# Expert loop of a mixture-of-experts block: a gate chunk split ahead of the rows, and the result rows copied by one engine

## The reference, cut to what matters

```
def hier_moe(h, ...):                 # 512 tokens, D = 1024
    g_sel = argmax(h @ w_rg + b_rg)   # 4 groups
    top_v, top_i = top_k(e_logit of that group's 8 experts, 2)
    gate = softmax(top_v) * g_p
    ...                               # tokens sorted by expert, blocks of 128 rows
    def expert_block(xb, e):          # 32 experts, inner width 512
        return (silu(xb @ w_gate[e]) * (xb @ w_up[e])) @ w_down[e]
    out[token] += expert_block(...) * gate
x = x + hier_moe(rms_norm(x), ...)
```

## Time and profile before

| | |
|---|---|
| median of 3 runs | 3697.85 us (3696.06 to 3704.15) |
| profiled execution | 3699.9 us |
| its span, first to last instruction | 3698.1 us |
| PE busy | 3507.7 us, 95% |
| DVE busy | 2201.3 us, 60% |
| ACT busy | 1511.9 us, 41% |
| POOL busy | 423.4 us, 11% |
| moved by DMA | 522.35 MB, mean 141 GB/s |

### The profile page before, as it was taken

The page is one execution under the profiler, slowest core; times in us unless marked ns, Lnnn a source line. Parts: engine busy times, 40 slices in busy tenths (PEclk is TensorE's granted clock), DMA queues, the critical chain, the costliest instruction groups (busy, mean ns, idle before and its releaser), DMA issues. The chain is left out here.

```text
span 3698.1 us, 44707 instructions
## 1 busy us (share of the span) xinstructions
PE 3507.7 (95%) x17472; PEld 2876.0 (78%) x17472; DVE 2201.3 (60%) x2966; ACT 1511.9 (41%) x1709; POOL 423.4 (11%) x315
## 2 busy tenths in 40 slices
PE   8999999899899999999999999899997997999998
PEld 6888888655888888888758888877876866887786
DVE  7545446538654467557897433653226326999998
ACT  4111111547422232223445222544545235777775
POOL 2000000200110011001111100100000011444442
PEclk9999999999999999999999999999999997999999
DMA  6323323210244335444212232231222226999997
GB/s 258 122 81 104 113 89 102 65 57 1 80 148 137 117 100 182 154 153 149 69 33 68 94 103 83 72 130 52 86 86 74 92 82 227 355 355 352 357 369 299
DMA packets 315240, 522.35 MB, mean 141 GB/s; under 512 B 18516, under 2 KB 274561, under 8 KB 289216
## 3 DMA queue, kind: packets, MB, share of 16 engines
q1 hardware_dynamic: 304032, 507.06, 39.9%
q0 software_dynamic: 11040, 12.91, 1.1%
HBM read 519.91 MB, written 25.17 MB: 147 GB/s over the span
## 5 line engine op out<-in xcount | busy, mean ns | idle before, releaser
L531 PE MATMUL banks<-operand_hi,trunk_weights_hi 128*128 128x512 f32 (+1 forms) x1568 | 569.2, 363 | 32.8 <-DVE operand_lo L1088 10.7
L531 PE MATMUL banks<-operand_lo,trunk_weights_hi 128*128 128x512 f32 (+1 forms) x1568 | 559.9, 357 | 0.0
L531 PE MATMUL banks<-operand_hi,trunk_weights_lo 128*128 128x512 f32 (+1 forms) x1568 | 559.6, 357 | 0.0
L531 PEld LDWEIGHTS banks<-operand_hi,trunk_weights_hi 128*128 128x128 f32 x1568 | 300.5, 192 | 81.3 <-issue 29.7
L531 PEld LDWEIGHTS banks<-operand_hi,trunk_weights_lo 128*128 128x128 f32 x1568 | 300.6, 192 | 41.7
L531 PEld LDWEIGHTS banks<-operand_lo,trunk_weights_hi 128*128 128x128 f32 x1568 | 300.7, 192 | 41.2 <-issue 0.5
L4249 DVE TENSOR_TENSOR ex_w_lo<-weight_ring,ex_w_hi 128x2048 fp32r<-128x2048 f32 x128 | 288.9, 2291 | 41.5 <-ACT ex_w_hi L4181 41.5
L1316 DVE TENSOR_TENSOR trunk_weights_lo<-weight_ring,trunk_weights_hi 128x2048 fp32r<-128x2048 f32 x90 | 206.4, 2294 | 177.2 <-ACT trunk_weights_hi L1271 177.2
L1271 ACT ACTIVATE trunk_weights_hi<-weight_ring 128x2048 fp32r<-128x2048 f32 x90 | 171.7, 1907 | 216.5 <-PE banks L531 216.3
L4181 ACT ACTIVATE ex_w_hi<-weight_ring 128x2048 fp32r<-128x2048 f32 x128 | 241.7, 1913 | 22.1 <-PE banks L4089 22.1
L531 PE MATMUL banks<-trunk_hidden_hi,trunk_weights_hi 128*128 128x512 f32 (+1 forms) x672 | 233.4, 347 | 4.6 <-DVE X L1818 2.1
(11 more groups left out here) (612 smaller groups left out, 7394.5 us busy)
## 6 DMA issues: line engine op xcount, KB each, us to landing
weight_ring<-ffn_w SPq DMA_DIRECT2D x120, 1024.0 KB, 5.2
weight_ring<-w_mod SPq DMA_DIRECT2D x72, 1024.0 KB, 5.1
weight_ring<-w_gate SPq DMA_DIRECT2D x64, 1024.0 KB, 6.8
weight_ring<-w_up SPq DMA_DIRECT2D x64, 1024.0 KB, 7.6
room<-w_down SPq DMA_DIRECT2D x64, 1024.0 KB, 7.1
weight_ring<-w_in SPq DMA_DIRECT2D x26, 1024.0 KB, 5.2
weight_ring<-ffn_w SPq DMA_DIRECT2D x16, 768.0 KB, 4.5
weight_ring<-o_w_pw SPq DMA_DIRECT2D x8, 1024.0 KB, 5.4
```

What stands on the lines that cost most here:

```text
L531: ins = pe.matmul(bank[:, at:at + width], w, x[:, at:at + width], start=start and n == 0, stop=stop and n == len(passes) - 1)
```

## The change

In `step`, ACT splits GATE0 of the next expert straight behind UP1, then the turned token rows, then GATE1, and only then copies the result rows, all 1024 columns in one instruction. DVE's copy of Y and its semaphore go; DVE makes the low part of GATE0 ahead of that of the token rows. PE's order in the step is the same.

For expert 0 the two UP chunks go to the slots (2, 1) in place of (1, 2), so that UP0 has a free slot from the start and UP1 waits for the gate product; the two halves of its matrix change places with that. The transposes of X and the copies to `XR` move from ahead of the loop to behind it, around the last `turn_h`; ACT alone copies them, in five banks in turn, and DVE waits for them before its first addition.

```
-def load_expert_chunk(k, sp, c, e):
-    half = c % 2
+FIRST_UP = (2, 1)
+def load_expert_chunk(k, sp, c, e, other=0):
+    half = (c + other) % 2
...
-        XRT = lambda j: k.PS[3 - j // 2][:, 512 * (j % 2):512 * (j % 2) + 512]
+        XRT = lambda j: (k.PS[0][:, 0:512], k.PS[0][:, 512:], k.PS[3][:, 512:], G, U)[j % 5]
...
 # POOL, scatter
                 pool.wait_ge(s_ya, m * 2 + (u + 2))
-                pool.wait_ge(s_yd, m * 2 + (u + 2))
...
 # PE: the transposes of X leave the start of the block, and
             step(n, 1, more=False)
+            for j in range(3):
+                turn_rows(j)
             turn_h(n, 2)
+            for j in range(3, 2 * ST):
+                if j >= 5:
+                    pe.wait_ge(s_xra, j - 4)
+                turn_rows(j)
             down(n, 2, DOWN[0])
...
 # ACT
             def rows_out(m, u):
                 act.wait_ge(s_mm, nth(m, u, DOWN[1]))
                 act.wait_ge(s_free[(u + 1) % 2], m + (u - 1) // 2 + 1)
-                act.activation(YS[:, (u + 1) % 2, 0:512], Y[:, 0:512], ACT.Copy).then_inc(s_ya, 1)
+                act.activation(YS[:, (u + 1) % 2, :], Y[:], ACT.Copy).then_inc(s_ya, 1)
...
                 chunk_hi(m, u, UP[1])
+                if more:
+                    chunk_hi(m, u + 1, GATE[0])
+                    turned_x(m, u + 1)
+                    chunk_hi(m, u + 1, GATE[1])
                 rows_out(m, u)
-                if more:
-                    turned_x(m, u + 1)
-                    chunk_hi(m, u + 1, GATE[0])
-                    chunk_hi(m, u + 1, GATE[1])
                 chunk_hi(m, u + 1, DOWN[0], 1 if more else 3)
-            for j in range(0, 2 * ST, 2):
-                act.wait_ge(s_xr, j + 1)
-                act.activation(XR[:, j // 2, 0:512], XRT(j), ACT.Copy).then_inc(s_xra, 1)
             chunk_hi(0, 0, GATE[0])
             chunk_hi(0, 0, GATE[1], 3)
             turned_x(0, 0)
-            chunk_hi(0, 0, UP[0])
+            chunk_hi(0, 0, UP[0], slot=FIRST_UP[0])
+            chunk_hi(0, 0, UP[1], slot=FIRST_UP[1], used=GATE[1] + 1)
             turned_x(0, 1)
             silu(0, 0)
-            chunk_hi(0, 0, UP[1])
...
             step(n, 1, more=False)
+            for j in range(3):
+                rows_of_x(j)
             turned_h(n, 2)
             chunk_hi(n, 2, DOWN[1])
+            for j in range(3, 2 * ST):
+                rows_of_x(j)
...
 # DVE
                 chunk_lo(m, u, UP[1])
-                rows_out(m, u)
                 if more:
+                    chunk_lo(m, u + 1, GATE[0])
                     turned_x(m, u + 1)
-                    chunk_lo(m, u + 1, GATE[0])
                     chunk_lo(m, u + 1, GATE[1])
...
             for t in range(ST):
+                dve.wait_ge(s_xra, 2 * t + 2)
                 dve.wait_ge(s_y[t], 16)
```

More of the change, by code:

```diff
@@ L3747, in _ @@
             for c in (*GATE, *UP):
-                load_expert_chunk(k, sp, c, 0)
+                load_expert_chunk(k, sp, c, 0, other=int(c in UP))
             for t in range(ST):
@@ L3988, in experts @@
         sem = lambda n: k.sem(f"ex_{n}")
-        s_hi, s_lo, s_mm, s_xt, s_xh, s_xl, s_silu, s_he, s_ht, s_hh, s_hl, s_ya, s_yd = (
+        s_hi, s_lo, s_mm, s_xt, s_xh, s_xl, s_silu, s_he, s_ht, s_hh, s_hl, s_ya = (
             sem("w_hi"), sem("w_lo"), sem("products"), sem("x_turned"), sem("x_hi"), sem("x_lo"), sem("silu"), sem("hidden"),
-            sem("h_turned"), sem("h_hi"), sem("h_lo"), sem("y_act"), sem("y_dve"))
+            sem("h_turned"), sem("h_hi"), sem("h_lo"), sem("y_out"))
         s_xg, s_ys = [sem(f"gathered{i}") for i in range(2)], [sem(f"scattered{i}") for i in range(2)]
-        s_tok, s_id, s_go, s_xr, s_xra, s_xrd = sem("tokens_now"), sem("ids_now"), sem("go"), sem("x_rows"), sem("x_rows_act"), sem("x_rows_dve")
+        s_tok, s_id, s_go, s_xr, s_xra = sem("tokens_now"), sem("ids_now"), sem("go"), sem("x_rows"), sem("x_rows_act")
         s_free = [sem(f"rows_free{i}") for i in range(2)]
@@ L4098, in turn_x, with up @@
                 ins.then_inc(s_xt, 1)
-            def up(bank, m, u, c, count=1):
+            def up(bank, m, u, c, count=1, slot=None, first=0):
                 pe.wait_ge(s_lo, nth(m, u, c))
-                hi, lo = (w[:, c % 3, :].rearrange("p (k n) -> p k n", k=4) for w in (w_hi, w_lo))
+                slot = c % 3 if slot is None else slot
+                hi, lo = (w[:, slot, :].rearrange("p (k n) -> p k n", k=4) for w in (w_hi, w_lo))
                 for i in range(4):
-                    kk = 4 * (c % 2) + i
-                    ins = three(bank, (x_hi[:, u % 2, kk, :], x_lo[:, u % 2, kk, :]), (hi[:, i, :], lo[:, i, :]), kk == 0, kk == KD - 1)
+                    kk = 4 * ((c + first) % 2) + i
+                    ins = three(bank, (x_hi[:, u % 2, kk, :], x_lo[:, u % 2, kk, :]), (hi[:, i, :], lo[:, i, :]),
+                                c % 2 == 0 and i == 0, c % 2 == 1 and i == 3)
                 ins.then_inc(s_mm, count)
@@ L4119, in down @@
                     pe.wait_ge(s_ya, m * 2 + u)
-                    pe.wait_ge(s_yd, m * 2 + u)
                 hi, lo = (w[:, c % 3, :].rearrange("p (k n) -> p k n", k=2) for w in (w_hi, w_lo))
@@ L4141, in step, with turn_rows @@
                 up(U, m, u, UP[1], 1 if more else 3)
-            for j in range(2 * ST):
+            def turn_rows(j):
                 t, half = divmod(j, 2)
@@ L4146, in _ @@
                 ins.then_inc(s_xr, 1)
-            pe.wait_ge(s_xra, ST)
-            pe.wait_ge(s_xrd, ST)
             turn_x(0, 0)
@@ L4153, in _ @@
             turn_x(0, 1)
-            up(U, 0, 0, UP[0])
-            up(U, 0, 0, UP[1])
+            up(U, 0, 0, UP[0], slot=FIRST_UP[0], first=1)
+            up(U, 0, 0, UP[1], slot=FIRST_UP[1], first=1)
             n = last_pair(pe)
@@ L4174, in _, with chunk_hi @@
             act.sem_inc(s_ya, 1)
-            def chunk_hi(m, u, c, count=1):
+            def chunk_hi(m, u, c, count=1, slot=None, used=None):
                 turn = u if c in DOWN else u + 1
+                slot = c % 3 if slot is None else slot
                 act.wait_ge(landed[c], m * 32 + 16 * turn)
-                if not isinstance(m, int) or m or u or c > 2:
+                if used:
+                    act.wait_ge(s_mm, used)
+                elif not isinstance(m, int) or m or u:
                     act.wait_ge(s_mm, nth(m, u, c - 3))
-                act.activation(w_hi[:, c % 3, :], raw[c], ACT.Copy).then_inc(s_hi, count)
+                act.activation(w_hi[:, slot, :], raw[c], ACT.Copy).then_inc(s_hi, count)
             def turned_x(m, u):
@@ L4222, in _ @@
             turned_x(0, 0)
-            chunk_hi(0, 0, UP[0])
+            chunk_hi(0, 0, UP[0], slot=FIRST_UP[0])
+            chunk_hi(0, 0, UP[1], slot=FIRST_UP[1], used=GATE[1] + 1)
             turned_x(0, 1)
             silu(0, 0)
-            chunk_hi(0, 0, UP[1])
             chunk_hi(0, 1, GATE[0])
-            chunk_hi(0, 1, GATE[1])
+            chunk_hi(0, 1, GATE[1], used=nth(0, 0, UP[1]))
             chunk_hi(0, 1, DOWN[0])
@@ L4233, in _, with rows_of_x @@
                 step(m, 2)
+            def rows_of_x(j):
+                act.wait_ge(s_xr, j + 1)
+                act.activation(XR[:, j // 2, 512 * (j % 2):512 * (j % 2) + 512], XRT(j), ACT.Copy).then_inc(s_xra, 1)
             step(n, 1, more=False)
+            for j in range(3):
+                rows_of_x(j)
             turned_h(n, 2)
             chunk_hi(n, 2, DOWN[1])
+            for j in range(3, 2 * ST):
+                rows_of_x(j)
             act.wait_ge(s_mm, nth(n, 2, DOWN[1]))
@@ L4243, in _, with chunk_lo @@
         def _(dve):
-            dve.sem_inc(s_yd, 1)
             dve.sem_inc(s_hl, 1)
-            def chunk_lo(m, u, c, count=1):
+            def chunk_lo(m, u, c, count=1, slot=None):
                 dve.wait_ge(s_hi, nth(m, u, c))
-                dve.tensor_tensor(w_lo[:, c % 3, :], raw[c], w_hi[:, c % 3, :].bitcast(F32), ALU.subtract).then_inc(s_lo, count)
+                slot = c % 3 if slot is None else slot
+                dve.tensor_tensor(w_lo[:, slot, :], raw[c], w_hi[:, slot, :].bitcast(F32), ALU.subtract).then_inc(s_lo, count)
             def turned_x(m, u):
@@ L4267, in turned_h @@
                                   ALU.subtract).then_inc(s_hl, 1)
[L4269 to L4272, removed]
             def step(m, u, more=True):
@@ L4285, in step @@
                 chunk_lo(m, u + 1, DOWN[0], 1 if more else 3)
-            for j in range(1, 2 * ST, 2):
-                dve.wait_ge(s_xr, j + 1)
-                dve.tensor_copy(XR[:, j // 2, 512:1024], XRT(j)).then_inc(s_xrd, 1)
             chunk_lo(0, 0, GATE[0])
@@ L4291, in _ @@
             turned_x(0, 0)
-            chunk_lo(0, 0, UP[0])
+            chunk_lo(0, 0, UP[0], slot=FIRST_UP[0])
+            chunk_lo(0, 0, UP[1], slot=FIRST_UP[1])
             turned_x(0, 1)
-            chunk_lo(0, 0, UP[1])
             chunk_lo(0, 1, GATE[0])
```

## The result

The changed kernel is slower: median 3713.03 us (3709.23 to 3718.92, 8 runs) against 3696.70 (3691.95 to 3704.15, 8 runs), ratio 1.0042 with a 95% interval of 1.0033 to 1.0051. I had forecast 3680.5 and a range of 3673 to 3689. The profiled execution has a span of 3717.1 us (3698.1 before); it is the slowest of the eight, so it shows the loss rather large.

The account below looks back on a forecast made before the run. PE was taken to bound the loop, losing time only in waits for DVE. Loop -11.4, start -6.7 and end +0.7 gave -17.4 us from the median 3697.85: 3680.5 us, range 3673 to 3689.

Parts of the forecast that it names:

- The loop on PE, ACT and DVE: Expert loop: PE's two waits for DVE shrink, gaining 0.38 us a period, 11.4 us over 30 periods.
- GATE0's wait: Loop: PE's wait for GATE0's low part from DVE, 7.0 us in 28 times, would go, with 0.4 to 0.5 us to spare.
- hidden's: Loop: PE's wait for the hidden rows from DVE would fall to about 0.24 us from 0.59 a step.
- The 128x1024 copy of Y: Loop, ACT: one copy of 1024 columns, taken as 1.03 us from the token rows' copy; cost put at nothing.
- The scatter starts some 4 us later: Loop, POOL: later scatter and next gather, rows used one and a half steps later; cost put at nothing.
- my signs of being wrong: ACT waits for a landing, SyncE's waits for DVE go, or PE waits for the token rows' low part.
- the rivals: Half the loop's gain lost, 3686.4 (0.14); no loop gain, transfers or DVE bounding, 3691.9 (0.11); slower, 3713 (0.05).
- The slower one: Loop: GATE0's buffer freed late, its landing delays ACT, PE waits for token rows; 0.7 us a period, 3713, chance 0.05.
- Transfers: Loop: weight transfers stay off the path, though a shorter period asks for 366 GB/s; the trace shows 417 GB/s.
- the 11.4 us: The loop's forecast gain, 30 periods at 0.38 us, with ends of 9.3 and 13.2.
- The start: Start of the block: without the transposes and copies, the first `turn_h` comes 6.7 us earlier, ends 4.3 and 8.
- The end: End of the block: ACT's copies of X delay DVE's last additions, costing 0.7 us, ends 0 and 2.

Follow-up runs that it names:

- gather_ahead: Changed kernel, with POOL's program reordered so that a gather never stands behind the scatter of the same step: median 3687.77 us, ratio 0.9967.
- gather_then_scatter: From tokens_ahead, gather and scatter change places behind the one wait for Y, so the gather is issued first: median 3679.01 us, ratio 0.9948.
- tokens_ahead: Changed kernel, with POOL's copy of the next gather's tokens ahead of the wait for Y, the gather still behind the scatter: median 3710.84 us, ratio 1.0033.

## Why the prediction was wrong

*The loop on PE, ACT and DVE: right.* I had 18.19 - 0.38 = 17.81; with the gathers in time it is 17.81 in three kernels. GATE0's wait is gone, and hidden's is 8.5 / 27 = 0.31 a step (0.24 forecast). The 128x1024 copy of Y takes 1.00 to 1.03 us, as taken from the token rows' copy. In gather_ahead steps of 17.69 to 17.74 and 17.86 to 17.91 alternate in place of 18.13 to 18.26.

*"The scatter starts some 4 us later, and behind it in POOL's order the next gather; its rows are used one and a half steps later, so I cost that at nothing too": this step failed.* I had named the queue and then counted the wrong gather. A gather issued behind the scatter of one step is the one that the next step's `turn_x` needs, 11.0 us after its issue and not one and a half steps. It landed 16.6 us after the last `turn_x`, in a period of 18.2. Both numbers were in the trace, in POOL's timeline and in the median landing; I did not lay them side by side. The "some 4 us" were right: Y is copied 4.4 us later. The gather is issued 4.9 us later, since POOL takes 0.5 more from there (1.44 and 2.26 for the scatter and the token copy in place of 1.02 and 2.02, less a shorter hand-over). The landing then took 6.6 in place of 9.4, and still came too late. The term that I had put at nothing cost 36.4 us in the profiled executions, 570.8 against 534.4 with the same loop and its gathers in time, or 1.2 us a period; PE's weight load waits 31.3 us for `x_slots` in 25 of these steps. None of my signs of being wrong named the gather.

*None of the rivals was it.* The slower one had the right shape, a landing with a late release that PE pays in each step, and its place, GATE0's weights, was wrong. What told the two apart was slack: 1.6 us against 6.6 by the prediction's own numbers (13.6 less a landing of 7). That its time, 3713, is the measured median is luck: the 0.7 us a period in it was assumed, for another transfer.

*Transfers: right.* The faster loops move 363 to 365 GB/s at a share of 0.97, in the stretch from 3130 to 3640. The Trainium skill ("DMA: Bandwidth & Descriptors", "Specifications") has about 358 as one core's limit; by that figure nothing of the 11.4 us would have come. Here, with one core streaming alone, it did.

*The start: right in kind.* 5.7 us in place of 6.7. The gather landed 3.31 us after its issue, GATE0 of expert 0 starts at 3084.08, 10.4 us behind `slot_tokens`, and the clock did not fall again behind the later stalls: PE waited 1.05 us ahead of 3096.57 and 1.61 ahead of 3101.19 (0.9 and 1.85 forecast), and the granted clock is 1.00, the higher level, in every slice of 2 us from 3092 to 3108. In the kernel before it was 0.50 behind a stall of 3.52. The eight transposes at half clock took 1.98 us, where the estimate was 1.6. The lines:

```profile
3074.46 3.71 ACT L4189 ACTIVATE ex_w_hi<-weight_ring 128x2048 fp32r<-128x2048 f32 x2 [14.06 <-PEq L3697]
...
3096.91 1.91 ACT L4189 ACTIVATE ex_w_hi<-weight_ring 128x2048 fp32r<-128x2048 f32 x1
```

```profile
3076.38 3.31 DMA x_slots<-normed_rows,tokens_now
...
3084.08 7.82 PE banks L4089 x24
...
3096.57 3.03 PE banks L4089 x12
3099.64 0.04 issue
3099.68 1.92 ACT ex_w_hi L4189
```

*The end: right.* +0.9 for +0.7. DVE's additions start at 3698.65, behind the last `ex_w_lo` at 3695.78. That one waited for an `ex_w_hi` of ACT that stood behind the three copies of X's rows (compare):

```profile
3695.78 2.29 DVE L4261 TENSOR_TENSOR ex_w_lo<-room,ex_w_hi 128x2048 fp32r<-128x2048 f32 x1 [0.78 <-ACT ex_w_hi L4189]
...
3698.65 10.15 DVE L4319 SCALAR_TENSOR_TENSOR x_rows<-weight_ring,gates,x_rows 128x1024 f32<-128x1024 f32 x8
```

## What to carry to other kernels

Before an instruction is moved back, follow what it releases until something lands or is used, through every queue, and write down the slack at the end of that chain; a wait that never shows in the profile may still be 1.6 us away from showing. Where a store waits for late work, issue the next load ahead of it; here that was enough although both stood behind the same wait. And a median landing is worth as much as a duration when a transfer is part of a circle.

## What the runs showed of the hardware that I had not expected

Two indirect transfers issued on POOL's queue behind each other did not overlap here: issued 1.76 us apart (tokens_ahead), their packets started about 3 us apart, and the first ones moved some 4 to 5 us after the issue. Why the lag is that long was not tried.

The time of POOL's small copies depends on what DVE does meanwhile. In gather_then_scatter both copies of one column take 0.2 us, in the 0.55 us in which DVE waits:

```profile
3315.55 0.20 POOL L4042 COPY tokens_now<-slot_tokens 128x1 uint32 x1
3315.68 0.18 POOL L4060 COPY ids_now<-slot_ids 128x1 uint32 x1
```

```profile
3315.82 2.29 DVE L4270 TENSOR_TENSOR ex_w_lo<-room,ex_w_hi 128x2048 fp32r<-128x2048 f32 x1 [0.55 <-ACT ex_w_hi L4198]
```

In the changed kernel the same copy, begun at 3326.71 beside a subtraction of DVE that began at 3326.65 and took 2.28, lasts 2.26: it ends as DVE's instruction ends. The Trainium skill, "SBUF — State Buffer", "🔬 SBUF: two separate sides", has a rule that fits: VectorE with two operands in SBUF and GpSimd share a pair of ports under an exclusive lock, and the later one waits for the whole instruction. By that rule POOL's place among DVE's instructions, not its own work, decides 2 us of a gather's way.
